# Norm sums gathered from cross products at three seams, and the first four tiles of the wide product run step by step

## The chip, the cores and the metric

One core of one Trainium2 chip runs the whole program. The metric is the device time of one launch in microseconds (us), lower is better. The engines are named as in the profile: PE is TensorE's matmul, PEld its weight load, DVE is VectorE, ACT is ScalarE, POOL is GpSimd, and SP is the queue that issues the loads.

## What is computed

The reference is a stack of transformer-like layers on 512 latent tokens of width 1024 (the first layer also carries 256 context tokens). Three places of it matter here. In each of them a product `y` is normed and added to the residual `x`, and the new `x` is normed again and multiplied by a wide matrix:

```
def rmsnorm(x, g):
    xf = x.astype(F32)
    y = xf * lax.rsqrt(jnp.mean(xf * xf, axis=-1, keepdims=True) + RMS_EPS)
    return (y * g.astype(F32)).astype(x.dtype)
...
        x = x + g1 * rmsnorm(y_lat, norm_g[l, 1])
        f_lat = swiglu(rmsnorm(x, norm_g[l, 2]) * (1.0 + sc2) + sh2, ffn_w_in[l], ffn_w_out[l])
        x = x + g2 * rmsnorm(f_lat, norm_g[l, 3])
```

Call such a place a seam. Seam A joins the first mixer's output product (`w_ab_out`) to the wide product `w_f0u`, seam B joins `w_att_out` to `w_f1u`, and seam C joins `w_f1d` to `w_ssm`. The second norm needs the mean of the squares of the new x, with x' = x + g·r·y (g the gain, r the reciprocal root of the first norm): mean(x'²) = mean(x²) + 2r·mean(g·x·y) + r²·mean(g²y²).

## The kernel before

Channels lie on the 128 partitions, in 8 blocks (`ND`), and tokens along the free dimension (512, `TL`). A sum over channels is therefore a matmul with a matrix of ones. Every product is computed as three fp32r matmuls per 128x128 block of weights: high part by high part, high by low, low by high.

**The products.** A wide product is a `Gemm` (line 219). Its weights arrive in chunks of 128 output channels; SP loads a chunk into one of four `w_raw` buffers, POOL splits it into a high part (`tensor_scalar`, line 284) and a low part (`tensor_tensor`, line 286), and PE runs 24 matmuls of 512 columns on it. There are two split buffers (`w_hi[0:2]`, `w_lo[0:2]`), and a third pair, `third`, for the third chunk of a product. Chunks go in turns of four (`RAW`), and tile n of a turn is accumulated in PSUM bank n. `split_done` counts the chunks split, `chunk_done` the chunks multiplied, `mm_free` the tiles whose bank has been read. The output product ahead of a seam is an `OutGemm` (line 395): 8 tiles, split by POOL at lines 450 and 454, multiplied at lines 482 to 484 (for seam A also 488 to 490, the context's 256 columns). Its tail object says what ACT and DVE do with each finished tile.

**The start of a wide product.** Where it follows a seam (`gate_k`), `first_pair` (line 295) runs the first two tiles step by step: for each block k it waits until h_hi and h_lo of that block are there, and runs the six matmuls of the two tiles. Tiles 3 and 4 follow whole (lines 337 to 339). At line 318 a tile waits until its bank is free. POOL splits the third chunk first, ahead of the first two (line 269), as soon as all but two of the chunks before are multiplied.

**The tail at seams A and B** (`NormAddTail`, line 656). During the output product, `SquareSum` (line 543) lets ACT square each tile into `wk` (line 562), DVE adds the squares up (line 568: `wk<-wk,wk`, and at seam A also `csq<-csq,csq` for the context), and ACT copies the tile to `y` and frees the bank. After the last tile PE sums over channels (lines 574, 577), ACT makes `rstd` (lines 679, 680), DVE scales and adds eight blocks to x (lines 705, 708), ACT squares each new block (line 686), PE sums each one with ones (line 694), ACT makes the second rstd (lines 688, 689), and then `Apply` runs per block: DVE scales (line 871), ACT makes h_hi (line 887), DVE makes h_lo (line 878).

**The tail at seam C** (`NormAddGainTail`, line 711) leaves the second rstd out of h: per block DVE scales (746), adds (749) and makes h_lo (752), ACT makes h_hi (733) and squares (736), and PE sums the square (`sum_tile`, line 725) between the matmuls of `first_pair`. The rstd is applied to each tile when it leaves PSUM (line 2444). `DtSide` runs a small product of 24 matmuls (line 2513) on PE after the fourth tile; it waits for `dtw_lo`, which DVE makes (line 2563) after it has taken the first tile.

**Behind seam A** DVE has other work before it takes the first tile: `RowsSide.dve_first` (line 1028) adds the context's residual, eight times a scale (line 1032) and an add (line 1035) on 256 columns. Only then does `Swiglu.dve` gate the first pair (line 1850), ACT round it (1842), and DVE make the low part and free two banks (line 1852).

## Time and profile before

| what | us |
|---|---|
| median of 3 runs | 3261.74 (3261.27 to 3262.06) |
| the profiled execution, its own time | 3263.07 |
| its span, first to last instruction | 3261.3 |
| PE busy | 3180.9 (98% of the span) |
| DVE busy | 1564.4 (48%) |
| POOL busy | 1662.9 (51%) |
| ACT busy | 914.3 (28%) |

The mean granted clock of TensorE over the span is 0.993 of full speed. A share of busy time is an average: at the seams PE runs in pieces and waits in between, and these stretches are what the change touches. Times below are microseconds from the start of the span. The "chain" is the chain of work that ended last: each piece was released by the piece before it.

### The profile page before, as it was taken

The numbers are of one execution on the slowest core, as the hardware profiler recorded it, in microseconds if no ns is written. First come the engines' busy times: TensorE is split into PE (matmuls) and PEld (weight loads), VectorE is DVE, ScalarE is ACT, GpSimd is POOL, SyncE is SP. The second block draws the span as 40 slices with busy tenths as digits, with TensorE's granted clock in tenths as the row PEclk, the third lists the DMA queues.
The fourth block names the chain that finished last, engine by engine and source line by source line (L and its number), as shares of the span: only waits on it lengthen the run. The fifth ranks groups of instructions, "written<-read, shape, count | busy, mean of one in ns | idle before, by whom it ended". The sixth has DMA issues, their size and how long they took to land.

```text
span 3261.3 us, 41273 instructions
## 1 busy us (share of the span) xinstructions
PE 3180.9 (98%) x15832; PEld 2603.2 (80%) x15832; DVE 1564.4 (48%) x2382; ACT 914.3 (28%) x1662; POOL 1662.9 (51%) x880
## 2 busy tenths in 40 slices
PE   8999999999999998999999999999999999999998
PEld 4889878888999755888868877788888788888886
DVE  5878668712333863111047667525531456645521
ACT  3122331111453453111022355322211214722210
POOL 2550036665887404566645633466666563056664
PEclk9999999999999999999999999999999999999999
DMA  5640027632554101233222311133332232023331
GB/s 220 203 133 14 14 72 251 238 109 88 154 178 152 59 1 58 81 94 108 98 67 87 95 46 40 59 91 96 96 106 90 91 92 72 8 91 96 96 106 69
DMA packets 84553, 319.31 MB, mean 98 GB/s; under 512 B 9200, under 2 KB 10864, under 8 KB 83376
## 3 DMA queue, kind: packets, MB, share of 16 engines
q1 hardware_dynamic: 84400, 317.20, 30.1%
q8 instruction: 105, 1.72, 0.2%
q14 instruction: 48, 0.39, 0.0%
HBM read 315.06 MB, written 2.10 MB: 97 GB/s over the span
## 4 chain that ended last, share of the span: by engine, by line
PE 90%; DVE 4%; POOL 2%; ACT 2%; issue 2%; DMA 1%; SPq 0%; DVEq 0%; POOLq 0%; ACTq 0%
PE two L337 17%; PE two L339 17%; PE two L338 17%; PE two L482 7%; PE two L484 7%; PE two L483 7%; PE two L2151 1%; PE two L2131 1%; PE two L2733 1%; PE two L1531 1%; PE two L2719 1%; PE two L2735 1%; PE two L2734 1%; PE two L1534 1%; PE two L2299 1%
## 5 line engine op out<-in xcount | busy, mean ns | idle before, releaser
L337 PE MATMUL two<-h_hi,w_hi 128*128 128x512 f32 x2144 | 851.3, 397 | 1.0 <-DVE h_lo L2036 1.0
L339 PE MATMUL two<-h_hi,w_lo 128*128 128x512 f32 x2144 | 839.7, 392 | 0.0
L338 PE MATMUL two<-h_lo,w_hi 128*128 128x512 f32 x2048 | 802.2, 392 | 0.0
L286 POOL TENSOR_TENSOR w_lo<-w_raw,w_hi 128x1024 fp32r<-128x1024 f32 x298 | 729.7, 2450 | 33.3 <-ACT w_hi L361 10.1
L284 POOL TENSOR_SCALAR w_hi<-w_raw 128x1024 fp32r<-128x1024 f32 x278 | 298.8, 1075 | 751.8 <-issue 400.3
L337 PEld LDWEIGHTS two<-h_hi,w_hi 128*128 128x128 f32 x2144 | 403.7, 188 | 91.6 <-issue 3.8
L339 PEld LDWEIGHTS two<-h_hi,w_lo 128*128 128x128 f32 x2144 | 403.1, 188 | 91.0
L338 PEld LDWEIGHTS two<-h_lo,w_hi 128*128 128x128 f32 x2048 | 385.5, 188 | 82.7 <-issue 1.4
L450 POOL TENSOR_SCALAR w_hi<-w_raw 128x1408 fp32r<-128x1408 f32 (+1 forms) x105 | 133.4, 1270 | 524.7 <-PE two L484 423.2
L454 POOL TENSOR_TENSOR w_lo<-w_raw,w_hi 128x1408 fp32r<-128x1408 f32 (+1 forms) x111 | 335.3, 3022 | 24.4 <-DVE zx L2988 9.2
L482 PE MATMUL two<-hid_hi,w_hi 128*128 128x512 f32 x704 | 276.7, 393 | 0.0
L484 PE MATMUL two<-hid_hi,w_lo 128*128 128x512 f32 x704 | 275.5, 391 | 0.0
L483 PE MATMUL two<-hid_lo,w_hi 128*128 128x512 f32 x704 | 275.3, 391 | 0.0
L568 DVE TENSOR_TENSOR wk<-wk,wk 128x512 f32<-128x512 f32 (+1 forms) x36 | 44.2, 1228 | 305.2 <-ACT wk L562 305.1
L1850 DVE TENSOR_TENSOR two<-wk,two 128x512 f32<-128x512 f32 (+1 forms) x66 | 40.0, 607 | 305.0 <-PE two L339 275.2
L3036 DVE SCALAR_TENSOR_TENSOR wk<-two,vec,wk 128x511 f32<-128x511 f32 (+1 forms) x176 | 131.9, 749 | 97.8 <-ACT wk L3014 85.1
L484 PEld LDWEIGHTS two<-hid_hi,w_lo 128*128 128x128 f32 x704 | 132.3, 188 | 29.6
L483 PEld LDWEIGHTS two<-hid_lo,w_hi 128*128 128x128 f32 x704 | 132.4, 188 | 28.4
L482 PEld LDWEIGHTS two<-hid_hi,w_hi 128*128 128x128 f32 x704 | 132.4, 188 | 28.3
L964 DVE SCALAR_TENSOR_TENSOR ada_junk<-ada_raw,ada_c 128x1024 f32<-128x1024 f32 x64 | 105.5, 1701 | 20.0 <-DMA ada_raw<-ada 20.0
L3030 DVE TENSOR_TENSOR two<-two,rstd 128x512 f32<-128x512 f32 x88 | 61.1, 695 | 100.6 <-PE two L339 100.6
L3014 ACT ACTIVATE wk<-two,vec 128x512 f32<-128x512 f32 x88 | 60.6, 689 | 169.2 <-DVE two L3030 169.2
(547 smaller groups left out, 5554.4 us busy)
## 6 DMA issues: line engine op xcount, KB each, us to landing
w_raw<-w_f0u SPq DMA_DIRECT2D x88, 512.0 KB, 3.6
row_raw<-ada SPq DMA_DIRECT2D x48, 512.0 KB, 5.2
w_raw<-w_ssm SPq DMA_DIRECT2D x48, 512.0 KB, 3.6
w_raw<-w_f0d SPq DMA_DIRECT2D x32, 704.0 KB, 4.1
w_raw<-w_f1u SPq DMA_DIRECT2D x44, 512.0 KB, 3.5
w_raw<-w_f2u SPq DMA_DIRECT2D x44, 512.0 KB, 3.5
w_raw<-w_f3u SPq DMA_DIRECT2D x44, 512.0 KB, 3.5
ada_raw<-ada SPq DMA_DIRECT2D x32, 512.0 KB, 3.7
```

The costliest lines, as they stand in the source:

```text
L284: nc.gpsimd.tensor_scalar(hi[:, 0:self.kt], w_raw[j][:, 0:self.kt], 1.0, 1.0, ALU.mult, ALU.mult).then_inc(hi_done, 1)
L286: nc.gpsimd.tensor_tensor(lo[:, 0:self.kt], w_raw[j][:, 0:self.kt], hi[:, 0:self.kt].bitcast(f32), ALU.subtract).then_inc(split_done, 1)
L337: nc.tensor.matmul(dst, w_h[:, k], hi, start=kk == 0, stop=False)
L338: nc.tensor.matmul(dst, w_h[:, k], lo, start=False, stop=False)
L339: last = nc.tensor.matmul(dst, w_l[:, k], hi, start=False, stop=kk == self.parts * self.kt - 1)
L450: nc.gpsimd.tensor_scalar(hi, raw, 1.0, 1.0, ALU.mult, ALU.mult).then_inc(hi_done, 1)
L454: nc.gpsimd.tensor_tensor(lo, raw, hi.bitcast(f32), ALU.subtract).then_inc(split_done, 1)
L482: nc.tensor.matmul(self.out(t), w_h[:, k], hi, start=kk == 0, stop=False)
L483: nc.tensor.matmul(self.out(t), w_h[:, k], lo, start=False, stop=False)
L484: last = nc.tensor.matmul(self.out(t), w_l[:, k], hi, start=False, stop=kk == self.parts * self.kt - 1)
L964: nc.vector.scalar_tensor_tensor(self.bufs.junk[v][:], self.bufs.raw[j][:], 1.0, self.bufs.c[:, v], ALU.mult, ALU.mult, accum_out=mods[sel ...
L3036: nc.vector.scalar_tensor_tensor(wk[n][:, back:TL], g.out(n)[:, 0:TL - back], self.col(i, n, j), wk[n][:, back:TL], ALU.mult, ALU.add).the ...
```

## The change

The three tails become one class, `SeamTail` (seam A: `BothSeamTail`). While the output product runs, ACT also squares each tile with the gain applied, and DVE also adds those squares up, multiplies each tile by its gain and by x (the cross product), and adds the cross products up. PE sums both accumulators after the last tile (`pe_end`), and DVE works out the sum of squares of the new x from the old one, kept in `x_sum2` (`total`). The squares of the new x, their eight matmuls and `Apply` are gone; at seams A and B one loop of DVE does scale, add, norm and h_lo per block. `x_sum2` is first filled by a copy at the start and again in the side work before seam B.

In `Gemm`, `first_quad` takes the place of `first_pair` at the three seams: the first pair of tiles runs step by step as before, the second pair two steps behind it (`LAG`). Two split buffers of their own (`own`) hold chunks 3 and 4, and POOL splits these two first. At seams A and B the low part of the second chunk waits until the last gained square is added (`own_after`). DVE's `sel` moves one turn later, and `dtw` lies elsewhere.

```diff
+        fourth = (arena("fourth_hi", [P, 8, P], 128 * K, f32r), arena("fourth_lo", [P, 8, P], 140 * K, f32r))
+        fourth0 = (arena("fourth0_hi", [P, 8, P], 140 * K, f32r), arena("fourth0_lo", [P, 8, P], 90 * K, f32r))
+        LAG = 2
...
-                        late = self.third_ahead and isinstance(i, int) and i == 1 and j < SPL
-                        sp.wait_ge(split_done, self.chunk0 + RAW * i + j + (2 if late else 1))
+                        late = self.quad and isinstance(i, int) and i == 1 and j < SPL
+                        sp.wait_ge(split_done, self.chunk0 + RAW * i + j + (1 + RAW - SPL if late else 1))
...
+                    seam = self.quad and isinstance(i, int)
+                    for at_, j in enumerate((*range(SPL, RAW), *range(SPL)) if seam and i == 0 else range(RAW)):
...
+                        if seam and i == 0 and j >= SPL:
                             pool.wait_ge(chunk_done, self.chunk0)
+                        elif self.third and isinstance(i, int) and n == SPL:
+                            pool.wait_ge(chunk_done, self.chunk0 + SPL)
+                        elif seam and i == 1 and j < SPL:
+                            pool.wait_ge(chunk_done, self.chunk0 + SPL + j + 1)
...
+                        if seam and n == SPL - 1 and self.own_after:
+                            pool.wait_ge(*self.own_after)
...
+                def first_quad():
+                    pe.wait_ge(split_done, RAW + self.chunk0 + RAW)
...
+                    for k in range(self.kt + LAG):
+                        if k < self.kt:
+                            pe.wait_ge(*self.gate_k(k))
+                            pair(k, range(SPL))
+                        if k >= LAG:
+                            pair(k - LAG, range(SPL, RAW))
...
+            def act(self, g, act, t):
...
                 self.sum.act(act, t, g.out(t))
+                if t >= 3:
+                    act.wait_ge(*upto(self.gsq_added, t - 2))
+                if t < ND - 1:
+                    nc.scalar.activation(self.gsq(t)[:], g.out(t), ACT.Square, scale=self.gain(t)).then_inc(self.gsq_ready[0], 1)
+                ins = nc.scalar.copy(y[:, t], g.out(t))
+                if t == ND - 1:
+                    ins.then_inc(self.y_copied[0], 1)
+                    act.wait_ge(*upto(self.y_copied, 1))
+                    ins = nc.scalar.activation(self.gsq(t)[:], y[:, t], ACT.Square, scale=self.gain(t))
+                    ins.then_inc(self.gsq_ready[0], 1)
...
+            def dve(self, g, dve, t):
+                self.sum.dve(dve, t)
+                if t >= 2:
+                    self.add_gsq(dve, t - 1)
+                dve.wait_ge(*(upto(self.y_copied, 1) if t == ND - 1 else upto(self.y_ready, t + 1)))
+                dst = self.cross_buf[t % 2] if t else self.cross_acc
+                sig(nc.vector, nc.vector.scalar_tensor_tensor(dst[:], y[:, t] if t == ND - 1 else g.out(t), self.gain(t), x[:, t], ALU.mult, ALU.mult), self.crossed)
+                if 0 < t < ND - 1:
+                    dve.wait_ge(*g.tile_read(t - 1))
+                    nc.vector.tensor_tensor(self.cross_acc[:], self.cross_acc[:], dst[:], ALU.add).then_inc(mm_free, 1)
...
+                elif self.shift is not None:
+                    dve.wait_ge(*g.tile_read(t - 1))
+                    nc.vector.tensor_tensor(self.cross_acc[:], self.cross_acc[:], dst[:], ALU.add).then_inc(self.cross_added[0], 1)
+                    self.add_gsq(dve, t)
...
+            def pe_end(self, pe):
+                last = ND - 1
+                if self.shift is None:
+                    pe.wait_ge(*upto(self.crossed, ND))
+                    nc.tensor.matmul(ps[4][:], ones[:], self.cross_acc[:], start=True, stop=False)
+                    nc.tensor.matmul(ps[4][:], ones[:], self.cross_buf[last % 2][:], start=False, stop=True)
...
+                    nc.tensor.matmul(ps[5][:], ones[:], self.gsq_acc[:], start=True, stop=False)
+                    nc.tensor.matmul(ps[5][:], ones[:], self.gsq(last)[:], start=False, stop=True).then_inc(self.summed[0], 1)
+                else:
+                    pe.wait_ge(*upto(self.cross_added, 1))
+                    nc.tensor.matmul(ps[4][:], ones[:], self.cross_acc[:], start=True, stop=True)
+                    pe.wait_ge(*self.all_added)
+                    nc.tensor.matmul(ps[5][:], ones[:], self.gsq_acc[:], start=True, stop=True).then_inc(self.summed[0], 1)
...
+            def total(self, dve):
+
+                dve.wait_ge(*upto(self.summed, 1))
+                sig(nc.vector, nc.vector.scalar_tensor_tensor(self.sum_buf[:], ps[5][:], 1.0 / D, rstd[:], ALU.mult, ALU.mult), self.steps)
+                sig(nc.vector, nc.vector.scalar_tensor_tensor(ps[5][:], ps[4][:], 2.0 / D, self.sum_buf[:], ALU.mult, ALU.add), self.steps)
+                sig(nc.vector, nc.vector.tensor_tensor(ps[5][:], ps[5][:], rstd[:], ALU.mult), self.steps)
+                sig(nc.vector, nc.vector.tensor_tensor(x_sum2[:], ps[5][:], x_sum2[:], ALU.add), self.steps)
+                sig(nc.vector, nc.vector.tensor_scalar(x_sum2[:], x_sum2[:], 0.0, None, ALU.max), self.steps)
...
+                self.total(dve)
+                scale(0)
+                add(0)
+                dve.wait_ge(*upto(self.rstd_ready, 2))
+                for k in range(ND):
+                    dve.wait_ge(*upto(self.added, k + 1))
+                    nc.vector.scalar_tensor_tensor(self.step_buf[k % 2][:], x[:, k], self.next_gain(k), self.x_rstd[:], ALU.mult, ALU.mult).then_inc(self.normed[0], 1)
+                    scale(k + 1)
+                    dve.wait_ge(*upto(self.hi, k + 1))
+                    nc.vector.scalar_tensor_tensor(h_lo[:, k], self.step_buf[k % 2][:], self.shift(k), h_hi[:, k].bitcast(f32), ALU.add, ALU.subtract).then_inc(self.lo[0], 1)
+                    add(k + 1)
```

At seam C (`shift is None`) `dve_end` keeps the order scale, add, h_lo, and runs `total` after the eighth block. In `BothSeamTail` ACT makes the context's reciprocal root (`c_rstd`, which `dve_first` waits for) in `act_last`, after its last h_hi; before, it did so right after the first rstd.

## Rows read from the trace of the kernel before

**Rows 1.** The page: the chain that ended last, shares by engine.
```profile
PE 90%; DVE 4%; POOL 2%; ACT 2%; issue 2%; DMA 1%; SPq 0%; DVEq 0%; POOLq 0%; ACTq 0%
```

**Rows 2.** The chain around seam A: start us, us, what.
```profile
449.45 1.29 PE two L574 x4
...
455.82 10.33 PE two L694 x16
...
470.19 0.76 PE two L304
...
494.67 0.23 PE two L337
```

**Rows 3.** The chain around seam B, same columns.
```profile
1280.42 0.86 PE two L574 x2
...
1297.21 0.70 ACT rstd L688
...
1298.66 0.76 DVE wk L871
...
1300.34 0.76 DVE h_lo L878
...
1301.23 0.77 PE two L304
...
1314.02 0.23 PE two L337
```

**Rows 4.** The chain around seam C, same columns.
```profile
1665.57 0.86 PE two L574 x2
...
1673.36 0.77 PE two L304
...
1704.01 5.55 PE two L2513 x24
```

**Rows 5.** Line 568 (sums of squares): duration ns min/median/max, first and last start.
```profile
L568 DVE TENSOR_TENSOR wk<-wk,two x12: 676/677/679, 2458.3 to 2881.5; 128x512 f32<-128x512 f32 x12
L568 DVE TENSOR_TENSOR csq<-csq,csq x6: 2498/2514/2516, 401.9 to 443.0; 128x256 f32<-128x256 f32 x6
```

**Rows 6.** Timelines of POOL and DVE near the output products' ends: start, us.
```profile
434.32 2.72 POOL L454 TENSOR_TENSOR w_lo<-w_raw,w_hi 128x1024 fp32r<-128x1024 f32 x1
...
1276.93 1.49 POOL L284 TENSOR_SCALAR w_hi<-w_raw 128x1024 fp32r<-128x1024 f32 x1
...
1280.87 1.04 POOL L284 TENSOR_SCALAR w_hi<-w_raw 128x1024 fp32r<-128x1024 f32 x1
...
1652.08 3.55 POOL L454 TENSOR_TENSOR w_lo<-w_raw,w_hi 128x1408 fp32r<-128x1408 f32 x1
...
1275.66 1.85 DVE L568 TENSOR_TENSOR wk<-wk,wk 128x512 f32<-128x512 f32 x1 [4.48 <-ACT wk L562]
```

**Rows 7.** DVE's timeline in the loop of seam C.
```profile
1671.74 0.68 DVE L749 TENSOR_TENSOR x<-x,wk 128x512 f32<-128x512 f32 x1
1672.46 0.75 DVE L752 SCALAR_TENSOR_TENSOR h_lo<-x,vec,h_hi 128x512 fp32r<-128x512 f32 x1
1673.12 0.75 DVE L746 SCALAR_TENSOR_TENSOR wk<-y,gains,rstd 128x512 f32<-128x512 f32 x1
```

**Rows 8.** Behind seam A: timelines of DVE and of POOL.
```profile
480.41 0.88 DVE L1032 SCALAR_TENSOR_TENSOR wk<-yc,gains,rstd_y 128x256 f32<-128x256 f32 x2
...
485.31 2.61 DVE L1035 TENSOR_TENSOR xc<-xc,wk 128x256 f32<-128x256 f32 x1
...
492.26 0.69 DVE L1852 TENSOR_TENSOR hid_lo<-two,hid_hi 128x512 fp32r<-128x512 f32 x1 [0.72 <-ACT hid_hi L1842]
...
485.19 2.44 POOL L286 TENSOR_TENSOR w_lo<-w_raw,w_hi 128x1024 fp32r<-128x1024 f32 x1
```

**Rows 9.** Behind seam C: DVE's timeline.
```profile
1699.86 2.67 DVE L2563 TENSOR_TENSOR dtw_lo<-dtw,dtw_hi 128x256 fp32r<-128x256 f32 x1 [1.09 <-ACT dtw_hi L2529]
```

**Rows 10.** A stretch of seam A: length, busy us (x instructions) of PE, PEld, DVE, ACT, POOL, PEclk, DMA share, GB/s.
```profile
474.00:475.00 1.00, 1.00 (x3) 0.73 (x3) 0.95 (x2) 0.72 (x1) 0.00 (x0) 0.50 0.00 0
```

More of the change, by code:

```diff
@@ L325, in turn @@
                             s = j % self.spl
-                            w_h, w_l = self.third if self.third and isinstance(i, int) and RAW * i + j == SPL else (s_hi[s], s_lo[s])
+                            w_h, w_l = self.split(i, j)
                             pe.wait_ge(split_done, RAW + self.chunk0 + RAW * i + j + 1)
@@ L689, in act_end @@
-                sig(nc.scalar, nc.scalar.activation(rstd[:], rstd[:], ACT.Exp, scale=-0.5), self.rstd_ready)
-            def pe_end(self, pe):
-                for k in range(ND):
-                    pe.wait_ge(*upto(self.sq_ready, k + 1))
-                    nc.tensor.matmul(ps[6][:], ones[:], wk[2 + k % 2][:], start=k == 0, stop=k == ND - 1).then_inc(self.sq_summed[0], 1)
-            def act_middle(self, act): pass
-            def dve(self, g, dve, t):
-                self.sum.dve(dve, t)
@@ L710, in build @@
-        class NormAddGainTail(NormAddTail):
-            def __init__(self, gain, next_gain):
-                super().__init__(gain)
-                self.next_gain = next_gain
-                self.hi, self.lo = cnt.take("h_hi_ready", ND), cnt.take("h_lo_ready", ND)
-            def tile_ready(self, k):
-                return upto(self.lo, k + 1)
-            def pe_end(self, pe): pass
-            def sum_tile(self, pe, k):
-                pe.wait_ge(*upto(self.sq_ready, k + 1))
-                nc.tensor.matmul(ps[6][:], ones[:], wk[2 + k % 2][:], start=k == 0, stop=k == ND - 1).then_inc(self.sq_summed[0], 1)
-            def act_end(self, act):
-                act.wait_ge(*self.sum.done)
-                astep(nc.scalar.activation(rstd[:], ps[6][:], ACT.Ln, bias=epsv[:, 0:1]))
-                sig(nc.scalar, nc.scalar.activation(rstd[:], rstd[:], ACT.Exp, scale=-0.5), self.rstd_ready)
-                for k in range(ND):
+                for k in range(ND if self.shift is None else 0):
@@ new lines, in act_end @@
+                astep(nc.scalar.activation(self.x_rstd[:], x_sum2[:], ACT.Ln, bias=epsv[:, 0:1]))
+                sig(nc.scalar, nc.scalar.activation(self.x_rstd[:], self.x_rstd[:], ACT.Exp, scale=-0.5), self.rstd_ready)
+                for k in range(0 if self.shift is None else ND):
+                    act.wait_ge(*upto(self.normed, k + 1))
+                    nc.scalar.activation(h_hi[:, k], self.step_buf[k % 2][:], ACT.Identity, bias=self.shift(k)).then_inc(self.hi[0], 1)
+                self.act_last(act)
@@ L3132, in ffn_add @@
             g = Gemm(up, 2 * NH, 1, 8, hrhs, evac_act=evac.act, evac_dve=evac.dve, gate_k=ap and ap.tile_ready, table=ACT.Silu, early=early,
[L3133 removed]
+                     own=(third, fourth) if ap else (), own_after=ap and ap.all_added, first_after=first_after)
             return product(tail, OutGemm(down, 2, KC, lambda k: (hid_hi[:, k], hid_lo[:, k]), tail, banks=(4, 5, 7, 3),
                                          k_gate=lambda k: (mm_free, NBANK + g.tile0 + 2 * k + 2), bank_gate=g.all_read))
[L3137 removed]
         rows1 = RowsSide(ada1, tail)
         sw = Swiglu(TL, hid_hi, hid_lo)
[L3140 removed]
+        gu = Gemm(w_f0u, 2 * NH, 1, 8, hrhs, evac_act=sw.act, evac_dve=sw.dve, gate_k=tail.tile_ready, table=ACT.Silu, side=rows1, peel=tuple(range(1, 11)),
+                  own=(third, fourth0), own_after=tail.all_added)
         tail = YTail(y, TL, ps[7])
@@ L3188, in build @@
         dt = DtSide(at_.done)
-        gm = Gemm(w_ssm, 32, 1, 8, hrhs, evac_act=sc.act, evac_dve=sc.dve, peel=(1, 2, 3, 4, 5, 6, 7), gate_k=r.tile_ready, table=ACT.Silu, side=dt, early=r, third=third)
+        gm = Gemm(w_ssm, 32, 1, 8, hrhs, evac_act=sc.act, evac_dve=sc.dve, peel=(1, 2, 3, 4, 5, 6, 7), gate_k=r.tile_ready, table=ACT.Silu, side=dt, own=(third, fourth))
         s = Ssd(gm, sc.out, dt)
```

209 lines of the change are left out of this document (132 added, 77 removed).

## The prediction

> **What bounds the kernel now.** I read the page first: PE holds 90% of the chain that ended last [rows 1], so only time in which PE stands still, or works on something that is not a product, can be won. Then the chain around each seam, where the reader is to see how long PE goes from the last matmul of one product to the fifth tile of the next. Seam A: the last output matmul ends at 449.45, PE's part in the sum of squares of the new x takes 10.33 us, the wide product starts at 470.19 and tile 5 at 494.67 [rows 2]. Seam B: 1280.42, start at 1301.23, tile 3 at 1314.02 [rows 3]; tiles 3 and 4 are 48 matmuls of 0.2285 us (seam A: 96 matmuls in 494.67 - 470.19, less the slow stretch, give the same), so tile 5 starts at 1325.0. Seam C: 1665.57, start at 1673.36, the small product at 1704.01 [rows 4].
>
> Last I looked at who else is busy there, in the timelines of DVE and POOL, and this decides my forecast. A DVE add with two SBUF inputs does not run beside a POOL instruction. The sum on line 568 takes 0.68 us with one input in PSUM, but its 256-column twin with both in SBUF 2.51 us [rows 5]. At 1275.66 DVE issues such an add; it ends at 1277.51, half a us after POOL has gone on to its next instruction at 1276.93, and that one takes 1.49 us where it takes 1.04 undisturbed, as at 1280.87 [rows 6]. So at each end of a POOL instruction one waiting DVE instruction gets through and holds POOL up by 0.45 us (256 columns: I take 0.25), and then DVE waits for a whole POOL instruction again.
>
> **What it removes.** At A and B the eight blocks through add, square and sum, and the second pass (Apply). At C the squares and eight sums on PE, 0.86 us each like the one at 1665.57 [rows 4], 6.9 us.
>
> **What it adds ahead of the wide product.** Per output tile ACT does one square more (0.5 us, in idle time) and DVE a cross product (one input in PSUM, so free), a cross add and a gained-square add, both with two SBUF inputs. In the middle of the product they hide: POOL rests between chunks. At its end they don't, since POOL splits chunks 3, 4 and 1 and the high part of chunk 2 in one go. A chunk is 1.04 [rows 6] + 2.44 us [rows 8], 3.5 with the gap.
>
> Seam B. POOL's last low part for the output product ends at 1273.4, held up by an add, so 1273.1 without it (one chunk, 3.5 us, ahead of the instruction at 1276.93 [rows 6]). From then on DVE has 9 such instructions to pass (three for tile 6, three for tile 7, and the last tile's cross product, cross add and square add), and POOL 3 x 3.5 + 1.04 = 11.5 us of work with 8 ends between. The last cross add gets through at 1273.1 + 11.5 + 8 x 0.45 = 1288.2 and ends at 1288.4; the last square add ends at 1289.1. `own_after` holds only the last low part. PE then needs 0.86 us a sum at full clock and twice that at half: both are summed between 1290.1 and 1292.0, I take 1291.0. `total` is five steps in a row, at 0.79 for two and 0.72 for three at most, 3.7 us: 1294.7. From the Ln of the rstd to PE's first matmul it took 1301.23 - 1297.21 = 4.02 us [rows 3], so PE starts at 1298.7, 2.5 us earlier. But the loop is slower per block. From norm to h_lo are 1.68 us (1298.66 to 1300.34 [rows 3]); an h_lo passes DVE in 0.66, an add with its wait in 0.72 [rows 7]: 3.07 us a block, against 2.74 for PE's twelve matmuls. The last h_lo is there at 1298.6 + 7 x 3.07 = 1320.1, PE has 24 matmuls left, 5.5 us, and tile 5 starts at 1325.7. **Seam B: +0.7.** With no DVE instruction held up, both sums are there at 1285.0 and tile 5 at 1319.6: -5.4 is the other end.
>
> Seam A. The same sum from 434.32 + 2.4 = 436.7 [rows 6], the hold-up of the add taken off: eight instructions (three with 256 columns) end the first sum of squares at 436.7 + 11.5 + 3.0 + 0.1 = 451.3, and four more go undisturbed, 2.95 us, to 454.3. PE's sums end at 455.5, `total` at 459.2, PE starts at 463.3 (6.9 us earlier), the last h_lo comes at 463.2 + 21.5 = 484.7, and the four tiles end at 490.2. Tile 5 needs the bank of tile 1, and DVE comes to that only after the context's residual: before, 480.41 to the low part's end at 492.95 [rows 8]. That took 10.4 us and 2.1 for the first pair; undisturbed it is 6.9, the rest is the wait for POOL, as the add of 2.61 us beside POOL's 2.44 shows. Now it starts at 484.7, since the last h_lo is later and `c_rstd` comes after ACT's last h_hi. POOL starts chunk 5 at 485.5 and chunk 6 right behind it, with its buffers free at once: 7 us and four ends, in which five of the sixteen instructions pass. That ends at 493.3; eleven more at 0.43 make 498.0, the first pair 500.1. So PE waits from 490.2 to 500.1, and tile 5 starts 5.4 us later than before. After a pause PE's clock was 0.50 at 474 to 475, half of full, the 1.2 GHz level [rows 10], with matmuls of 0.43; that cost about 2 us in the start of seam A (twelve matmuls 0.2 slower). I add 2. **Seam A: +7.4.** The other end has no hold-up at all: first h_lo 1.8 us earlier, context and pair 9.0 us, tile 5 at 491.9, -2.8, and 1 for the clock, -2.
>
> Seam C. From 1652.08 + 3.2 = 1655.3 [rows 6], again without its hold-up, POOL has four chunks, 14 us, and nine DVE instructions pass at its ends (here the first two scales too, as `own_after` is not set): 1655.3 + 14.0 + 8 x 0.45 = 1672.9. The second scale ends at 1673.4; an add, a scale, an add and an h_lo, 0.72 + 0.66 + 0.72 + 0.75 [rows 7], put the first h_lo at 1676.2 where it was 1673.2, and PE starts at 1676.4. The two-block lag and no sums let it end four tiles at 1700.3, not 1704.01. But the small product waits for `dtw_lo`. The rstd now comes after `total`, 1.4 us later than before, and the instruction, which took 2.67 us beside POOL instead of 0.42 [rows 9], issues at 1701.3 and waits again for the end of chunk 6, 1702.7: PE goes on at 1703.0. **Seam C: -1.0.** With no hold-up it is 1699.3, -4.7.
>
> The copy of `x_sum2` at the start (0.6 us on ACT) lies under the loads of the first weights, and the copy before B is side work: nothing; without that cover 0.6. The loads of chunks 5 and 6 wait for the third and fourth split, done over 20 us before use; nothing is queued behind them that is due sooner. Moved `sel` (0.19 us) is nothing either way.
>
> **Sum:** 7.4 + 0.7 - 1.0 = +7.1 on the profiled 3263.07, 3270.2. That execution stands 1.3 above the median, so the forecast is 3268.8.
>
> **The page on the hold-up.** The rows say a waiting add costs POOL 0.45 us. The Trainium skill, "SBUF — State Buffer", section "Who interferes with whom", says that a DVE instruction with two SBUF inputs and a GpSimd one that reads SBUF exclude each other for the whole instruction. By that each passage would cost 0.68, eight of them 1.8 us more at seam B; the measured 0.45 decides here.
>
> **The rivals.** (1) Faster: the one-at-a-time passage is mine from few rows. With POOL resting between its instructions, or several adds passing at once, the sums come early and the context's residual ends early: -2 - 5.4 - 4.7 = -12, 3249.7. For it: at seam A PE's part of 10.33 us does go away. Against: rows 5 and 6. Chance 0.21. (2) No change: the stall behind seam A stands (+5.4, no clock loss), but the hold-up counts half at B and C (-2.4, -2.9): 0, 3261.8. For it: `own_after` keeps POOL off the last adds. Chance 0.18. (3) Slower still: the clock. If PE is at half clock for the sums and well into the step loop at A and B, the two sums cost 1.7 more at each, and twelve matmuls take 5.1 us against the loop's 3.07, so three blocks at half clock lose up to 3 a seam: +7.1 + 6 = 3275. It decides once the half clock lasts beyond the second block. Against: before, it had risen again some 5 us after the start. Chance 0.08. That the change does less than it says I don't reckon with: the waits are plain in the code.
>
> **How the numbers follow.** My forecast has 0.53, of which 0.17 lies below +6.5 us. About 6.5 us, 0.2%, is what a measurement can tell from no change. Slower: 0.36 + 0.08 = 0.44; the same: 0.17 + 0.18 = 0.35; faster: 0.21. The forecast's own range is +1 to +10 (each seam 2 to 3 us). The range has to hold rival 1's centre and rival 3's: 3250 to 3274.
>
> **What would show it.** In the changed profile: the 256-column instructions of line 1032's kin ending near 498 and PE idle from about 490 to 500; tile 5 of seam B near 1325 plus the shift; DVE adds of 2 to 3 us with POOL beside them in the last two output tiles; a loop of 3.07 us a block; `dtw_lo` again long. Wrong if PE's idle time behind the four tiles of seam A is under 3 us, or if the seams' sums are there within 5 us of the last output matmul.

## The result, and the profile after

The changed kernel took 3269.02 us (median of 9 runs, 3264.08 to 3273.32), the kernel before in the same rounds 3262.06: a ratio of 1.0022, 95% interval 1.0012 to 1.0031. It is slower by about the least that can be told from no change. Measured again later beside other kernels it took 3264.78 (11 runs, 3263.37 to 3269.07), 1.0012 (1.0003 to 1.0021). The sign stands, the size lies between 2 and 7 us, and what sets that width is the subject of the last section.

The profiled execution is 3269.02 us too, with a span of 3267.1 (3261.3 before). Its page, the shares of the chain, beside [rows 1]:

```profile
PE 89%; DVE 5%; ACT 2%; issue 1%; POOL 1%; DMA 1%; SPq 0%; DVEq 0%; POOLq 0%; ACTq 0%
```

The waits of PE (line waited for: us in all, times, longest), of which these belong to the seams (the first row holds seams A and B, L853 is seam C):

```profile
PE two L335 <- DVE h_lo L865: 15.2, 3, 7.6
...
PE two L378 <- DVE hid_lo L1984: 9.0, 1, 9.0
...
PE two L797 <- DVE e_buf L773: 4.2, 2, 3.6
...
PE two L335 <- DVE h_lo L853: 3.2, 1, 3.2
...
PE two L2645 <- DVE dtw_lo L2695: 2.7, 1, 2.7
```

The reader is to see one new wait that is long and stands alone: 9.0 us on the low part of the first pair (L1984). It is behind seam A. The chain there, beside [rows 2] and [rows 8] (start us, us, what):

```profile
452.58 1.13 PE two L797 x2
...
458.08 0.76 DVE wk L835
...
482.69 0.88 DVE wk L1162 x2
...
485.09 2.55 DVE xc L1165
...
488.81 2.49 DVE xc L1165
...
494.75 0.44 DVE xc L1165
...
497.37 0.79 PE two L378
498.16 0.43 PE two L379
```

PE's part in the norm is gone (10.33 us before, now two sums, 2.0 us together), and the wide product starts at 462.18 instead of 470.19. But tile 5 starts at 497.37, 2.7 us later than before: from 488.3 PE stands still, until DVE is through the context's residual (L1162, L1165) and the first pair. And then it runs at half clock: PEclk is 0.53 from 490 to 500, a matmul takes 0.43. When ACT squares the first tile of the next output product, the program is 4.6 us behind the one before (756.81 against 752.20). Such a distance between the same instruction in two profiles is called the lag below.

Seam B, beside [rows 3]: DVE's timeline in the last two tiles, then POOL's (`e_buf<-y,gains,x` is the last tile's cross product, the other DVE rows are adds).

```profile
1277.19 1.68 DVE L768 TENSOR_TENSOR e_buf<-e_buf,e_buf 128x512 f32<-128x512 f32 x1
1278.80 1.52 DVE L609 TENSOR_TENSOR wk<-wk,wk 128x512 f32<-128x512 f32 x1
1280.35 2.78 DVE L780 TENSOR_TENSOR e_buf<-e_buf,e_buf 128x512 f32<-128x512 f32 x1
...
1284.56 2.87 DVE L609 TENSOR_TENSOR wk<-wk,wk 128x512 f32<-128x512 f32 x1
1287.46 1.41 DVE L780 TENSOR_TENSOR e_buf<-e_buf,e_buf 128x512 f32<-128x512 f32 x1
1288.90 2.72 DVE L765 SCALAR_TENSOR_TENSOR e_buf<-y,gains,x 128x512 f32<-128x512 f32 x1
1291.66 1.40 DVE L773 TENSOR_TENSOR e_buf<-e_buf,e_buf 128x512 f32<-128x512 f32 x1
```

```profile
1278.29 1.49 POOL L291 TENSOR_SCALAR third_hi<-w_raw 128x1024 fp32r<-128x1024 f32 x1
1279.86 2.72 POOL L295 TENSOR_TENSOR third_lo<-w_raw,third_hi 128x1024 fp32r<-128x1024 f32 x1
1282.55 1.49 POOL L291 TENSOR_SCALAR fourth_hi<-w_raw 128x1024 fp32r<-128x1024 f32 x1
1284.13 2.75 POOL L295 TENSOR_TENSOR fourth_lo<-w_raw,fourth_hi 128x1024 fp32r<-128x1024 f32 x1
1286.85 1.49 POOL L291 TENSOR_SCALAR w_hi<-w_raw 128x1024 fp32r<-128x1024 f32 x1
1288.42 2.65 POOL L295 TENSOR_TENSOR w_lo<-w_raw,w_hi 128x1024 fp32r<-128x1024 f32 x1
1291.05 1.48 POOL L291 TENSOR_SCALAR w_hi<-w_raw 128x1024 fp32r<-128x1024 f32 x1
```

Each of the first six DVE instructions shown ends 0.4 to 0.6 us after a POOL instruction has begun: one is let through at each end. The seventh ends 0.5 us after POOL's last high part, behind which POOL waits for `own_after`. The sums start on PE at 1293.12 and run at half clock, the wide product starts at 1304.20, tile 5 at 1330.23. The program is 5.2 us behind when it comes to this seam. With that taken off, the product starts 2.2 us earlier than before, and tile 5 is within 0.1 us of the seam before (1325.0): the slower loop has used up the gain.

Seam C, beside [rows 4] and [rows 9] (chain):

```profile
1674.25 4.03 DVE wk L835 x2
...
1681.08 0.47 PE two L335
...
1705.08 2.47 DVE dtw_lo L2695
1707.59 2.49 PE two L2645 x10
```

The small product starts 3.6 us later than before, with 5.4 us brought along: the seam gives back 1.8. The end is 5.8 us later. So A costs 4.6, the copy ahead of B 0.6, B 0.2 at most, and C gives back 1.8 (1.6 as the state-space stage begins): 3.8 us behind when that stage ends, 2091.57 against 2087.79. The other 2.0 us are lost in code that the change does not touch, 1.5 right there and 0.5 behind 2850, both at short stretches of half clock.

### The profile page after: what moved, and what is told of

The parts are those of the page before. It is cut to its first block, busy times and chain, and to the rows that moved or that the text cites. A ratio compares the mean times of both kernels' runs of the same rounds, so it can differ in the third digit from the quotient of the medians.

```text
span 3267.1 us, 41281 instructions
## 1 busy us (share of the span) xinstructions
PE 3170.9 (97%) x15800; PEld 2595.6 (79%) x15800; DVE 1637.9 (50%) x2461; ACT 916.1 (28%) x1664; POOL 1660.0 (51%) x880
## 4 chain that ended last, share of the span: by engine, by line
PE 89%; DVE 5%; ACT 2%; issue 1%; POOL 1%; DMA 1%; SPq 0%; DVEq 0%; POOLq 0%; ACTq 0%
PE two L378 17%; PE two L380 16%; PE two L379 16%; PE two L523 7%; PE two L525 7%; PE two L524 7%; PE two L2283 1%; PE two L2263 1%; PE two L2865 1%; PE two L1663 1%; PE two L2867 1%; PE two L2866 1%; PE two L2851 1%; PE two L1666 1%; PE two L2431 1%
## 5 line engine op out<-in xcount | busy, mean ns | idle before, releaser
L378 PE MATMUL two<-h_hi,w_hi 128*128 128x512 f32 x2120 | 841.7, 397 | 10.0 <-DVE hid_lo L1984 9.0
L380 PE MATMUL two<-h_hi,w_lo 128*128 128x512 f32 x2120 | 830.5, 392 | 0.0
L379 PE MATMUL two<-h_lo,w_hi 128*128 128x512 f32 x2024 | 792.5, 392 | 0.0
L295 POOL TENSOR_TENSOR w_lo<-w_raw,w_hi 128x1024 fp32r<-128x1024 f32 x295 | 716.2, 2429 | 37.6 <-ACT w_hi L402 10.8
```

What stands on the lines that cost most here:

```text
L295: nc.gpsimd.tensor_tensor(lo[:, 0:self.kt], w_raw[j][:, 0:self.kt], hi[:, 0:self.kt].bitcast(f32), ALU.subtract).then_inc(split_done, 1)
L378: nc.tensor.matmul(dst, w_h[:, k], hi, start=kk == 0, stop=False)
L379: nc.tensor.matmul(dst, w_h[:, k], lo, start=False, stop=False)
L380: last = nc.tensor.matmul(dst, w_l[:, k], hi, start=False, stop=kk == self.parts * self.kt - 1)
```

## The experiments

Times are medians of 11 runs (8 in one case), to be read against 3262.3 to 3262.6 for the kernel before in the same rounds. The changed kernel's own median moves by 4 us between rounds (3269.02, later 3264.78), which is more than most of these changes are worth. So the argument rests on where events lie in the profiles, one for each version, and a median that meets an expectation can do so by luck. Line numbers of the variants are shifted.

**The residual behind the pairs.** The context's residual is computed two blocks at a time behind the first four pairs:

```diff
-                for k in range(ND + 1):
...
+            def residual(self, dve, h):
+                for k in range(2 * h, 2 * h + 3):
...
             def dve(self, dve, i, q):
+                if isinstance(i, int) and i < 2:
+                    self.residual(dve, 2 * i + q)
```

> Only the place of the context's residual at seam A changes: its sixteen DVE instructions no longer stand ahead of the first pair of the wide product, but four each behind the h_lo of the first four pairs. Theory (the residual ahead of the first pair is what tile 5 waits for): tile 5 starts where the four tiles end, at about 488.5 instead of 497.4, PE does not stand still there, and the second stretch at half clock (about 491 to 500) goes with it: 9 us and 1.5 us, so 10.5 us under the changed kernel, about 3258.5, which is also below the kernel before. Rival 1 (the wait only moves: the residual and the rows delay the second pair, and tile 7 stands still in its place): less than 4 us gained, a wait of PE on L1984 of over 4 us, now in front of tile 7 near 500. Rival 2 (the split of chunk 5, which starts on POOL only at 483.8, sets tile 5): tile 5 at 491 or later, about 6 us gained.

3259.77 us (3256.69 to 3263.09), 0.9994 (0.9985 to 1.0003). The two waits of PE in its timeline (in brackets: idle before, and on what):

```profile
488.69 0.51 PE L378 MATMUL two<-h_hi,w_hi 128*128 128x512 f32 x1 [0.33 <-DVE hid_lo L1988]
...
503.61 0.50 PE L378 MATMUL two<-h_hi,w_hi 128*128 128x512 f32 x1 [3.63 <-DVE hid_lo L1988]
```

The theory holds for tile 5: it starts 8.7 us earlier, when the four tiles end, and no half clock follows (PEclk is 1.00 from 485 to 505). Just behind it PE is 10.3 us ahead of the changed kernel, the 10.5 that were expected. But rival 1 is there as well: a wait of 3.6 us comes at tile 7, because residual and first rows now stand ahead of the second pair, and another us goes in small waits by 550. What is left is 5.6 us (ACT's square at 751.25 instead of 756.81), and seam B's product starts 5.8 us earlier (1298.39).

**POOL waits earlier.** At A and B the wait for the last adds goes from the low part of chunk 2 to ahead of chunk 1:

```diff
+                        if seam and n == 0 and self.own_after:
+                            pool.wait_ge(*self.own_after)
...
-                        if seam and n == SPL - 1 and self.own_after:
-                            pool.wait_ge(*self.own_after)
```

> At seams A and B POOL waits for the last adds ahead of chunk 1, not only ahead of the low part of chunk 2, so that after chunks 3 and 4 the adds meet no POOL instruction. Theory (DVE's adds are let through one at each end of a POOL instruction, and this is what makes the sums late): at B the last square add ends 3.4 us earlier (at 8 to 9 us behind POOL's last low part for the output product plus chunks 3 and 4) and PE's first matmul of the wide product too; at A the adds end about 1.9 us earlier, but the scale and the first adds of the step loop then lie beside POOL's chunks 1 and 2 and give back 0 to 1.9. Together 3.4 to 5.3 us under the changed kernel, about 3264.7. Rival (the adds wait for ACT's squares or for the output product itself, not for POOL): nothing is gained, and POOL's two chunks, now later, delay the four tiles by 0 to 3 us: 3269 to 3272.

3264.90 us (3262.10 to 3272.44), 1.0009 (1.0000 to 1.0018). DVE's timeline at the end of seam B's output product:

```profile
1288.07 0.69 DVE L780 TENSOR_TENSOR e_buf<-e_buf,e_buf 128x512 f32<-128x512 f32 x1
1288.80 0.75 DVE L765 SCALAR_TENSOR_TENSOR e_buf<-y,gains,x 128x512 f32<-128x512 f32 x1
1289.59 0.69 DVE L773 TENSOR_TENSOR e_buf<-e_buf,e_buf 128x512 f32<-128x512 f32 x1
```

Without POOL beside them the cross product and its add take 0.75 and 0.69 us, where they took 2.72 and 1.40. The adds end 2.8 us earlier and PE's product starts at 1302.02, 2.2 us earlier. It had come 0.6 us late to the sums, so B gains 2.8, not 3.4. At A the adds end 1.0 us earlier, but the first scale of the step loop now waits for POOL, 2.71 us at 457.20, and the product starts at 463.26, 1.1 us later. At A the wait moved the collision, it didn't remove it. The median meets the expected 3264.7, but that is no evidence: by the profiles A and B together give 1.7 us, and the changed kernel itself took 3264.78 when it was repeated.

**The old seam A.** Tail, second pass and first pair of the kernel before at A alone (no diff: it is the removed code of the change, for w_ab_out and w_f0u).

> Seam A as in the kernel before (old tail, second pass, first pair, no copy of the sum of squares at the start), seams B and C as in the changed kernel. Theory (A costs the changed kernel 5 to 5.6 us, B and the copy ahead of it cost 0.6 to 0.8, C gives back 1.6, and the last 1.5 us go in the product behind the state-space stage): 5.3 us under the changed kernel, 3263.7, some 1.7 above the kernel before. Rival (the loss is spread, or lies in the memory moves and the order of loads and not in A): within 2 us of the changed kernel. The runs of the changed kernel scatter over 9 us, those of the kernel before over 1.6: if A's stall is where the scatter comes from, it is gone here.

3262.66 us (3257.81 to 3263.54), 0.9999 (0.9990 to 1.0008): 6.4 under the first measurement of the changed kernel, 2.1 under the second. In the profile the product of seam B starts at 1300.09 instead of 1304.20, 4.1 us earlier, and the small product at 1703.73 instead of 1707.59, 3.9 us. So the loss is in A, as expected, at some 4 us of the 4.6 to 5.2 that the two profiles had given. Nine of its runs lie within 1.5 us, two 4 us lower. From lowest to highest that is 5.7 us, as in the repetition of the changed kernel, so the scatter does not go away with A.

**Two tiles in step instead of four.** The new sums everywhere, but the wide products begin as before.

> The new norm sums at all three seams, but the wide product begins with the old first pair (tiles 1 and 2 step by step, tile 3 and 4 whole behind them), POOL's order and waits as before. Theory (four tiles in step hide the slower step loop): at B two tiles end about 1.4 us after the last h_lo and two whole tiles of 5.5 us follow, where with four tiles 5.5 us follow the last h_lo: tile 5 is 6.9 us later. At A tile 5 waits for the context's residual anyway, at 497.4: 0, and as PE is busy until 494 there, the stretch at half clock is shorter, -1.5 to 0. At C the loop goes at 1.93 us a block, faster than four tiles can (2.74), so that most of it cancels: 0 to +2. Together about +6.5 on the changed kernel, 3275.5. Rival (the four tiles bring nothing, since the half clock eats the gain): within 2 us of the changed kernel.

3271.00 us (3267.43 to 3273.25), 1.0026 (1.0017 to 1.0035): 2.0 over the changed kernel's first median, 6.2 over its second, with 6.5 expected. Seam by seam, in the profiles: A is level (tile 5 comes 1.2 us later, at 498.58, but PE is busy until 496.4, there is no half clock behind it, and ACT's square comes at 756.55 instead of 756.81). At B tile 5 starts 32.8 us after the product's start instead of 26.0, 6.8 as expected, and 5.8 of it are left, since the product starts 1.0 us earlier. C gives back 3.7, where a loss of up to 2 was expected: the product starts 1.9 us earlier, counted from where the program stands, and the small product comes 24.7 us after it instead of 26.5. Together +1.8. PE's timeline in the loop at B shows why four tiles pay there:

```profile
1311.59 0.50 PE L521 MATMUL two<-h_hi,w_hi 128*128 128x512 f32 x1 [1.26 <-DVE h_lo L1041]
```

With two tiles PE idles 1.26 us of each 2.93 us block. At C a block takes DVE 1.93 us, and two tiles leave PE idle 0.3 us at most; there the four tiles in step end 23.8 us after their start, and what they win the wait of 2.73 us for `dtw_lo` takes away again (it took DVE 2.45 us there, 1.08 here).

**The residual spread further.** Two blocks ahead of the first pair, two each behind the second, third and fourth.

> As the first experiment, but the context's residual is spread so that no pair waits for it: two blocks of columns ahead of the first pair (in the idle time of DVE from 482.6 to 486.5), then two behind the second, third and fourth pair. Theory (what was left in the first experiment was the second pair, which waited behind residual and rows, and tile 7 with it, 3.6 us at 503.6): tile 5 still at 488.5, tile 7 at about 499.7 without a wait, 3.6 us under the first experiment and 9 + 3 under the changed kernel: about 3256. Rival (DVE as such has too much to do in these turns): the wait moves on to tile 9 or 11, and less than 1.5 us is gained on the first experiment.

3263.88 us (3258.09 to 3268.09), 1.0002 (0.9993 to 1.0011): the theory failed and the rival held. Tile 7 does not wait any more, tile 11 does, and a half clock follows (the matmul takes 0.79):

```profile
526.46 0.79 PE L378 MATMUL two<-h_hi,w_hi 128*128 128x512 f32 x1 [4.59 <-DVE hid_lo L1989]
```

The block behind the third pair took 4.7 us beside POOL (its two adds 3.08) and the four rows behind it 9.1, so the fourth pair was passed on at 526.4, with 521.9 wanted. An estimate of the room: a turn of four tiles takes PE 22.0 us (96 matmuls of 0.229), and of these DVE needs 13.7 for twelve row instructions of 1.14 us and 4.2 for two pairs; 4 us are left. They lie where four row instructions follow (behind the second and the fourth pair), not where eight do. At the next output product the program is at 753.54, 2.3 us behind the first experiment.

**dtw first.** At C dtw_hi and dtw_lo are computed in DVE's and ACT's idle time ahead of the first tile's evacuation.

```diff
+            def act_first(self, act):
+                act.wait_ge(phase_in, self.val)
+                nc.scalar.copy(dtw_hi[:, :, :], dtw[:, :, :]).then_inc(self.dtw_hi[0], 1)
+            def dve_first(self, dve):
+                dve.wait_ge(*upto(self.dtw_hi, 1))
+                nc.vector.tensor_tensor(dtw_lo[:, :, :], dtw[:, :, :], ...)
```

> Only seam C: dtw_hi and dtw_lo are computed ahead of the first tile's evacuation, when DVE is idle (1696.0 to 1700.2), and not behind it. Theory (at C the four tiles end at 1704.86 and the small product waits 2.73 us for dtw_lo, which stands beside POOL's split of chunk 6): the small product starts where the tiles end, 2.7 us under the changed kernel, 3266.3. Rival (the time is lost again at the next wait, for the bank of the first tile or in the state-space stage): the stage's end moves by less than 1 us.

3263.91 us (3262.36 to 3266.61), 1.0005 (0.9996 to 1.0014). The small product starts at 1704.5 with no wait ahead of it, 3.1 us earlier than in the changed kernel, and the state-space stage's sum 3.1 us earlier too (2088.47 against 2091.57): nothing is given back. The medians can't show it: 5.1 us under the changed kernel's first, 0.9 under its second.

**One input in PSUM at B.** The middle tiles' squares and cross products go to free banks; instructions and POOL's work stay.

```diff
-                self.sum = SquareSum()
+                self.sum = SquareSum(between=(1, 2) if psum else ())
...
-                ..., self.cross_buf = ..., b[4:6]
+                ..., self.cross_buf = ..., (ps[3], ps[3]) if psum else b[4:6]
```

> Only seam B: ACT writes the squares of tiles 2 to 7 and DVE the cross products into free PSUM banks, so that the adds of both have one input in PSUM; the number of instructions and POOL's work stay. Theory (only a DVE instruction with two SBUF inputs waits for POOL, and it holds POOL up in turn): four instead of nine instructions wait in the last tiles, the adds of lines 609 and 768 take 0.7 us beside POOL, and the sums are there some 3 us earlier, so that PE starts the wide product 3 us earlier: about 3266. Rival 1 (any DVE instruction waits beside POOL, or the adds are late because ACT's squares are): no change, 3269. Rival 2 (the adds hold POOL up even with an input in PSUM): the adds are short, POOL's instructions keep 1.49 and 2.7 us, and the gain is under 1 us.

3262.99 us (3258.92 to 3268.77), 1.0001 (0.9992 to 1.0010). DVE's and POOL's timelines, to be laid beside those of the changed kernel:

```profile
1283.19 0.69 DVE L768 TENSOR_TENSOR e_buf<-e_buf,two 128x512 f32<-128x512 f32 x1
1283.79 0.68 DVE L609 TENSOR_TENSOR wk<-wk,two 128x512 f32<-128x512 f32 x1
1284.51 2.20 DVE L780 TENSOR_TENSOR e_buf<-e_buf,e_buf 128x512 f32<-128x512 f32 x1
```

```profile
1282.62 1.05 POOL L291 TENSOR_SCALAR fourth_hi<-w_raw 128x1024 fp32r<-128x1024 f32 x1
1283.74 2.41 POOL L295 TENSOR_TENSOR fourth_lo<-w_raw,fourth_hi 128x1024 fp32r<-128x1024 f32 x1
1286.13 1.48 POOL L291 TENSOR_SCALAR w_hi<-w_raw 128x1024 fp32r<-128x1024 f32 x1
```

The adds with an input in PSUM take 0.69 and 0.68 beside POOL, and POOL takes 1.05 and 2.41 beside them; the one add that kept two SBUF inputs still waits, 2.20, and POOL's next instruction pays 0.43. The cross sum starts at 1288.93 instead of 1293.12 and the wide product at 1299.67 instead of 1304.20, 4.5 us earlier. The program comes to this seam 0.5 us later here, so the seam is 5.0 us shorter; the next two versions with this repair give 5.0 as well.

**The first three repairs together.** The spread residual, POOL's earlier wait at B alone, dtw first.

> The repairs together: residual spread at A, POOL's earlier wait at B alone (the second experiment lost 1.1 us at A and won 2.8 at B), dtw_hi and dtw_lo first at C. If the three causes are independent the gains add up: 12 + 2.1 to 2.8 + 2.7, so 17 us under the changed kernel, 3252, and 10 under the kernel before. If they share a bound (PE's clock after each pause, or the side work behind the seams), less than two thirds of it comes: above 3257.

3261.02 us (3256.64 to 3261.37), 0.9990 (0.9981 to 0.9999): 4 us above the 3257 up to which the gains could be called independent. The gains at B and C were there (product of B at 1298.67, 2.5 us before the spread version; no wait for dtw_lo), but A brought its 4.59 us wait at tile 11 along, here too.

**Better in all three places.** Three blocks of the residual ahead of the first pair, two behind the second, three behind the fourth; PSUM at B; dtw first.

> The changed kernel with all three repairs: at A three blocks of the residual ahead of the first pair, two behind the second and three behind the fourth (so that neither the second nor the fourth pair is late), at B the adds with one input in PSUM, at C dtw_hi and dtw_lo first. Theory (three independent causes): tile 5 of A at 488.5 and no wait of over 1 us up to 560, 9.4 us and more; B 4.5; C 2.7: 16 to 17 us under the changed kernel, 3252 to 3253, which beats both kernels by 9 us or more. Rival (DVE cannot carry residual and rows in the first two turns at all): a wait of 3 to 5 us somewhere between 499 and 540 as in both earlier versions, 3256 to 3257.

3253.94 us (3251.35 to 3257.43), 0.9974 (0.9965 to 0.9983): it beats both kernels. ACT's square comes at 749.70, 7.1 us before the changed kernel's and 2.5 before that of the kernel before. One wait is left behind seam A:

```profile
490.54 0.79 PE L378 MATMUL two<-h_hi,w_hi 128*128 128x512 f32 x1 [2.66 <-DVE hid_lo L1989]
```

Three blocks did not fit ahead of the first pair: the second scale (1.17 us) and the last two adds (3.81 together) waited for POOL, and tile 5 is 2 us later than foreseen. After it there is none up to 560, so DVE can carry residual and rows; the rival is out. Against the changed kernel the medians give 15.1 us by its first and 10.8 by its second, the profiles 15.3 where the state-space stage ends (2076.29 against 2091.57).

**PSUM at C too.** The same for the middle tiles at seam C.

> The version before it, and at seam C too the squares and cross products of the middle tiles in free PSUM banks. Theory (operands with two SBUF inputs are what delays): at C fewer DVE instructions stand ahead of the first scale, the first h_lo comes 1 to 2 us earlier, and the small product with it: 1 to 2 us under the version before it. Rival (at C the first h_lo waits for the rstd and for the scale beside POOL, not for the adds): no change.

3252.49 us (3250.02 to 3256.17, 8 runs), 0.9970 (0.9959 to 0.9980). The intervals of the two overlap. The profile has PE waiting 2.46 us for C's first h_lo instead of 3.24: 0.8 us, less than expected, since the first scale waits for the rstd and then beside POOL. It has the lowest median, but whether it is faster than the version before it stays open. In its profile w_f0u ran slower at full clock (last section).

**The old A with the repairs of B and C.**

> Seam A as in the kernel before, B with one input in PSUM, C with dtw_hi and dtw_lo first. Theory: the gains of B and C, 4.5 and 2.7, on the experiment with the old seam A (3262.7): 3255.5. If the old A is as good as the new one with its residual spread, this is level with the best version; if the cost of A in the changed kernel is only the residual, it is some 3 us above it.

3255.48 us (3253.96 to 3260.54), 0.9980 (0.9971 to 0.9989), as worked out. That is 1.5 us over the version with the new A repaired, with intervals that overlap; in the profiles that version is 2.5 us ahead (749.70 against 752.17). So at A the new sums are worth 1.5 to 2.5 us once the residual is spread, and the old seam was no bad choice. Most of what the change brought, once repaired, lies in B and C.

**The changed kernel again.**

> The changed kernel again, beside the others on one chip. Its nine runs went from 3264.1 to 3273.3 where the kernel before stays within 2 to 4 us. Theory (PE's clock falls to half in some executions and not in others at pauses of a few us far from the seams, 1.7 us each, and every kernel has these places): the scatter is there again, the shorter runs with the higher mean clock (0.993 against 0.989). Rival (the first runs were a chip's or a moment's): within 3 us. Median 3269 either way.

3264.78 us, with the scatter again: six runs from 3263.4 to 3264.8 with mean granted clocks of 0.992 and 0.993, five from 3267.2 to 3269.1 with 0.990 to 0.992. The median was not 3269; that part of the expectation failed.

## Why the prediction was right, and where it was not

It gave 3268.8, the first measurement 3269.02. The direction and the mechanism at A are earned, the agreement to 0.2 us is luck. The prediction's sum is +7.1 at the three seams. In the profiles the seams and the copy make +3.8. The 7.0 us between the first medians come out only with 2.0 more from half clock in code that the change does not touch, and with about 1 because the profiled execution of the kernel before stood 1.0 above its median and that of the changed kernel at its own. The second measurement, 3264.78, is inside the range but 4 us under the forecast.

The range was to hold the centres of rivals 1 and 3. By the prediction's own terms these are 3249.7 and 3275, both just outside 3250 to 3274.

**Seam A, +7.4: measured +4.6.** The mechanism was right in its order: PE starts early, the context's residual begins only behind the last h_lo, POOL splits chunks 5 and 6 beside it, PE stands still, then the half clock. The sizes were off in three small steps. The sums and `total` were over 1.1 us earlier (458.06, not 459.2). The loop took 2.93 us a block, not 3.07, 1.0 us in seven blocks: I had taken an add with its wait at 0.72, and 0.61 of it lay on the path. The residual and pair took 14.6 us, not 15.4. Together they put tile 5 at 497.4 and not at 500.1, 2.7 of the 2.8 us. The first experiment shows that the residual is the cause: with it taken from ahead of the first pair, tile 5 starts 8.7 us earlier. In the kernel before it stood there too, but hidden: tiles 3 and 4 ran whole behind the first pair, so that PE had 14.3 us of work left when the residual began (480.41 to 494.67), and in the changed kernel it has 5.7 (482.69 to 488.35). The clock term was 2 and measured 1.9.

**Seam B, +0.7: measured 0.0 to 0.2.** With 5.2 us brought along, the prediction's last cross add ends at 1293.6 and the product starts at 1303.9; the trace has 1293.07 and 1304.20. The passage of one waiting instruction at each end of a POOL instruction, taken from three rows [rows 6], held in all seven DVE rows shown above, and the PSUM run shows that the second SBUF input is what counts. The product starts 0.3 us later than by the sum, and the block's 0.14 us, seven times, brings tile 5 0.7 earlier (1330.23, 1330.9 by the sum).

The Trainium skill, "SBUF — State Buffer", section "Who interferes with whom", says that a DVE instruction with at most one SBUF input does not contend with GpSimd, and one with two does; by that the PSUM run had to free both engines. Its rows agree (0.69, and POOL at 1.05 and 2.41). By the same page the blocked side waits for the whole instruction, 0.68 here; POOL's instructions were 0.43 to 0.44 longer (1.48 and 1.49 against 1.05) at its high parts and about 0.3 at its low ones, so the measured price was the right one to take. Part of the 0.68 lies ahead of POOL's row: the held-up adds end 0.4 to 0.6 us after it has begun.

**Seam C, -1.0: measured -1.8.** The first h_lo passed a little earlier than worked out (PE at 1681.08, 1681.8 by the prediction's sum), and dtw_lo stood beside POOL again, 2.45 us. That it alone held the small product was right: done first, 3.1 us go.

**Costed at nothing.** The copy of x_sum2 ahead of B: the lag of the program grows from 4.6 to 5.2 us across that stage. I had named 0.6 as its price without cover. It is one instruction on ACT, in a stage where ACT also makes the high parts of the weights. The first line is of the kernel before, the others of the changed one:

```profile
938.19 1.05 ACT L361 CAST w_hi<-w_raw 128x1024 fp32r<-128x1024 f32 x1
```

```profile
941.51 0.59 ACT L1278 COPY x_sum<-two 128x512 f32<-128x512 f32 x1
942.11 1.28 ACT L1279 ACT_TABLE_LOAD   x1
943.40 1.05 ACT L402 CAST w_hi<-w_raw 128x1024 fp32r<-128x1024 f32 x1
```

ACT has no gap there, so the cast behind the copy is 5.2 us behind, where ACT's logarithm ahead of the copy is 4.6 behind (940.21 against 935.59), and at 965.62 PE waits 0.24 us for a low part made from such casts, where it did not wait before. The experiment with the old seam A keeps this copy, and its lag grows by the same 0.6 us. No version leaves the copy out, so that it is the whole cause is read from the traces and not tried.

**Not in the sum.** The 1.5 us at 2091 and the 0.5 behind 2850.

**The rivals.** Faster by undisturbed adds: at B the seven DVE instructions shown were all held up. No change by half a hold-up: the hold-up is whole. Slower by the clock inside the loop: the half clock ended at 466.5 at A, in the second block, and at 1309.9 at B, with the end of the second block. In these two blocks only the first pair runs, six matmuls in 2.6 us at half clock, which fits a block of 2.93; from the third on there are twelve, and PE's slack is 0.2 us a block at full clock. So it cost nothing in the loop, by little.

**The signs of being wrong.** PE's idle time behind the four tiles was 9.0 us, far over 3. The other sign was near at A: the sums end there 5.5 us after the last output matmul (449.04 to 454.56), with 5 named as the limit.

## What to carry to other kernels

Before work is moved out of a gap, look at what used to fill that gap's place: here a residual that had been hidden behind the third and fourth tile came to stand bare when these two were run in step with the first pair. An accumulation that must run beside GpSimd should have one operand in PSUM where banks are free: that alone gave 5.0 us at one seam, and three free banks were its price. Where an engine's queue is nearly full over several tiles, moving an instruction block moves the wait to a later tile; work out the due time of every pair, not only of the first.

## What the runs showed of the hardware

**A short half clock far from the change costs 0 to 2 us, and comes in one execution and not in the next.** PE waits 2.47 us for ACT at the end of the state-space stage in every kernel of this study. In the changed kernel's profile four matmuls behind it take 3.64 us, in that of its repetition 1.98:

```profile
2091.57 3.64 PE L2839 MATMUL two<-s_out,ones 128*128 128x512 f32 x4 [2.47 <-ACT s_out L2971]
```

```profile
2090.03 1.98 PE L2839 MATMUL two<-s_out,ones 128*128 128x512 f32 x4 [2.47 <-ACT s_out L2971]
```

The granted clock of the same two executions (length, busy us of PE, PEld, DVE, ACT, POOL, then PEclk, DMA share, GB/s), the changed kernel first:

```profile
2090.00:2094.00 4.00, 2.43 (x3) 1.17 (x4) 0.86 (x2) 1.23 (x2) 2.99 (x2) 0.69 0.00 0
2740.00:2750.00 10.00, 7.17 (x36) 6.01 (x35) 6.89 (x12) 3.16 (x10) 3.39 (x2) 0.84 0.36 105
2850.00:2860.00 10.00, 7.00 (x25) 5.25 (x23) 3.26 (x5) 3.59 (x6) 6.79 (x4) 0.83 0.27 70
```

```profile
2090.00:2094.00 4.00, 3.97 (x13) 2.41 (x14) 0.56 (x1) 1.32 (x2) 3.92 (x3) 1.00 0.21 68
2740.00:2750.00 10.00, 5.70 (x36) 4.76 (x35) 5.70 (x12) 5.53 (x20) 1.46 (x1) 1.00 0.15 52
2850.00:2860.00 10.00, 8.41 (x37) 6.93 (x38) 3.73 (x6) 4.05 (x7) 7.36 (x5) 1.00 0.30 105
```

The first profile has three such places and the second none. What they cost follows from the same instruction in both. At 2091.57 the first profile is 1.5 us behind the second (2090.03), and at DVE's next add to x 3.0 (2111.74 against 2108.73). At 2850.97, where DVE adds to x again (2847.93 in the second), it is still 3.0, and at the end 5.2 (span 3267.1 against 3261.9). So the place at 2091 cost 1.5 us and the one behind 2850 cost 2.2. The one at 2740, which lies between, cost nothing. PE has waits there in both executions (busy for 7.17 and 5.70 of the 10 us), which slower matmuls can fill; that this is the reason is argued, not tried. The remaining 1.5 are no matter of the clock (next paragraph). The same code, the same pause, and the clock falls or doesn't. The kernel before has two of these places in its profile, at 2740 and 2850, though its runs lie within 4 us; why its runs scatter less stays open.

**A product can run 2% slower at full clock.** In the stage of w_ssm, from 1715 to 1880, the repetition runs 740 matmuls, the first profile 729 and the kernel before 728, all with PEclk 1.00. So the repetition comes to the stage 0.7 us later than the first profile (small product at 1708.27 against 1707.59) and leaves it 1.5 us earlier (2090.03 against 2091.57): 2.2 us won at full clock. In the PSUM-at-C version w_f0u ran slower in the same way, 781 matmuls from 531 to 713 against 797 in the version before it, which is some 4 us. What sets it is open. Before and after have the same rate in w_ssm, so it is no part of their difference, but it is another part of the scatter, and a difference of one such stage is not to be explained by the code.
